# Second feed-forward stage as seven block products

## The reference

```
def swiglu(u, w13, w2):
    a, b = jnp.split(u @ w13, 2, axis=-1)
    return (jax.nn.silu(a) * b) @ w2

def half_ffn(h, shift, scale, gate, g_pre, g_post, w13, w2):
    u = modulate(rmsnorm(h, g_pre), shift, scale)
    return h + 0.5 * gate * rmsnorm(swiglu(u, w13, w2), g_post)
```

## Time and profile before

| | |
|---|---|
| median of three runs | 2694.71 us |
| the profiled execution | 2693.38 us, span 2691.5 us |
| TensorE busy | 2550.4 us, 95% |
| VectorE busy | 1322.4 us, 49% |
| GpSimd busy | 1311.0 us, 49% |
| ScalarE busy | 850.0 us, 32% |
| mean granted TensorE clock | 0.975 |

### The profile page before, as it was taken

The page is one execution under the profiler, slowest core; times in us unless marked ns, Lnnn a source line. Parts: engine busy times, 40 slices in busy tenths (PEclk is TensorE's granted clock), DMA queues, the critical chain, the costliest instruction groups (busy, mean ns, idle before and its releaser), DMA issues. The chain is left out here.

```text
span 2691.5 us, 36342 instructions
## 1 busy us (share of the span) xinstructions
PE 2550.4 (95%) x14266; PEld 2208.8 (82%) x14266; DVE 1322.4 (49%) x1908; ACT 850.0 (32%) x1373; POOL 1311.0 (49%) x499
## 2 busy tenths in 40 slices
PE   7999999998998999998999998989989999979997
PEld 5899998887898888786888877879878898867775
DVE  6445663468664652035111225364445144359997
ACT  5333331234212422024100114334422011128774
POOL 1444544542642067774778775655537776620000
PEclk8999999999999999998999998999999999989998
DMA  7664423314211022231222224110012322539994
GB/s 281 231 245 153 154 98 127 123 66 167 76 66 35 20 94 94 94 129 63 100 84 106 95 93 178 67 62 1 1 66 106 127 88 85 200 141 401 372 374 167
DMA packets 59197, 352.10 MB, mean 131 GB/s; under 512 B 7236, under 2 KB 8388, under 8 KB 26352
## 3 DMA queue, kind: packets, MB, share of 16 engines
q1 hardware_dynamic: 57472, 344.39, 34.2%
q0 software_dynamic: 1584, 5.78, 0.5%
HBM read 323.13 MB, written 30.72 MB: 131 GB/s over the span
## 5 line engine op out<-in xcount | busy, mean ns | idle before, releaser
L186 POOL TENSOR_TENSOR whi<-raw,one_col 128x2048 fp32r<-128x2048 f32 (+2 forms) x135 | 445.3, 3298 | 666.3 <-PE bank L206 559.6
L189 POOL TENSOR_TENSOR wlo<-raw,whi 128x2048 fp32r<-128x2048 f32 (+2 forms) x135 | 578.3, 4284 | 10.6
L4443 DVE TENSOR_TENSOR moe_wl<-moe_raw,moe_wh 128x2048 fp32r<-128x2048 f32 x84 | 189.6, 2284 | 3.4 <-ACT moe_wh L4377 3.0
L4377 ACT ACTIVATE moe_wh<-moe_raw 128x2048 fp32r<-128x2048 f32 x84 | 160.0, 1913 | 36.8 <-PE bank L4355 19.3
L204 PE MATMUL bank<-uh_b,whi 128*128 128x512 f32 x352 | 139.1, 395 | 7.8 <-DVE ul_b L1063 6.8
L205 PE MATMUL bank<-ul_b,whi 128*128 128x512 f32 x352 | 138.3, 393 | 0.0
L206 PE MATMUL bank<-uh_b,wlo 128*128 128x512 f32 x352 | 138.1, 392 | 0.0
L4292 POOL DMA_INDIRECT out_dram<-moe_y,moe_rows x7 | 6.7, 950 | 258.5 <-DVE moe_y L4507 258.5
L204 PE MATMUL bank<-fa_hh,whi 128*128 128x512 f32 (+1 forms) x352 | 119.5, 340 | 3.3 <-DVE fa_hl L1761 3.3
L205 PE MATMUL bank<-fa_hl,whi 128*128 128x512 f32 (+1 forms) x352 | 119.4, 339 | 0.0
L206 PE MATMUL bank<-fa_hh,wlo 128*128 128x512 f32 (+1 forms) x352 | 119.0, 338 | 0.0
(11 more groups left out here) (701 smaller groups left out, 7364.4 us busy)
## 6 DMA issues: line engine op xcount, KB each, us to landing
moe_raw<-moe_w_dram SPq DMA_DIRECT2D x84, 1024.0 KB, 7.3
cond_ring<-w_ada_dram SPq DMA_DIRECT2D x27, 1024.0 KB, 8.9
raw<-gu_a_dram SPq DMA_DIRECT2D x22, 1024.0 KB, 5.0
raw<-gu_b_dram SPq DMA_DIRECT2D x22, 1024.0 KB, 4.8
raw<-wqkv_dram SPq DMA_DIRECT2D x12, 1024.0 KB, 4.8
raw<-dn_a_dram SPq DMA_DIRECT2D x16, 704.0 KB, 4.0
raw<-dn_b_dram SPq DMA_DIRECT2D x16, 704.0 KB, 4.0
n_ada<-w_ada_dram SPq DMA_DIRECT2D x9, 1024.0 KB, 21.6
```

The source lines that it names most:

```text
L186: e.nc.gpsimd.tensor_tensor(e.whi[p][:, 0:f], e.raw[p][:, 0:f], e.one_col[:, 0:1].to_broadcast([P, f]), ALU.mult).then_inc(e.w_hi, 1)
L189: e.nc.gpsimd.tensor_tensor(e.wlo[p][:, 0:f], e.raw[p][:, 0:f], e.whi[p][:, 0:f].bitcast(F32), ALU.subtract).then_inc(e.w_split, 1)
L4377: nc.scalar.activation(wh[s % RING_W][:, :], raw[s % RING_RAW][:, :], ACT.Copy).then_inc(hi_done, 1)
L4443: nc.vector.tensor_tensor(wl[s % RING_W][:, :], raw[s % RING_RAW][:, :], wh[s % RING_W][:, :].bitcast(F32), ALU.subtract).then_inc(lo_done, 1)
```

## The change

The second stage is written as a new function, `ffn_seven_b`, with its own object of class `Seven`:

- The stream order is gu_b0, gu_b1, dn_b0, dn_b1. Slots 0 to 2 stay as they are, the other 19 are seven block products of 256 columns.
- Three weight sums are left on GpSimd (`pool_sums` is 3); the fourth is on VectorE (`dve_sum`). All seven low parts are on VectorE (`pool_lo` is empty).
- The norm writes its tiles over the residual XR (`over_x`), so that the token blocks are whole and can be summed in place.
- The first 11 gated tiles stay in SBUF (`fb_kept`, where `fb_hl` comes to lie), the other 11 go to `hid_b` in memory by way of two buffers, and come back tile by tile while the last down slot of the first half frees `fb_hl`.
- The kept tiles are split when the last gate-and-up slot is in work; the first down slot's weights are split by ScalarE and VectorE.

```diff
-          ("gu_b0", HTILES, 16), ("dn_b0", 8, HTILES), ("gu_b1", HTILES, 16), ("dn_b1", 8, HTILES),
+          ("gu_b0", HTILES, 16), ("gu_b1", HTILES, 16), ("dn_b0", 8, HTILES), ("dn_b1", 8, HTILES),
...
+        if over_x:
+            self.u = [self.x[:, k, 0:w] for k in range(KT)]
+        self.nu = len(self.u)
...
+            if self.pool_lo:
+                dve.wait_ge(self.lo_pool, 2 * i + 2)
...
+    def last_sum(self, eng, i):
+        return eng.tensor_tensor(self.block(i, 0), self.block(i, 1), self.s[1][:, :], ALU.subtract)
+    def dve_sum(self, dve, i):
+        dve.wait_ge(self.s_ready, self.pool_sums * i + 3)
+        dve.wait_ge(self.lo_part, self.lo_count(i, 0))
+        self.last_sum(self.e.nc.vector, i).then_inc(self.s_last, 1)
     def pool_slot(self, pool, i):
-        e, G, g, s = self.e, self.e.nc.gpsimd, self.first + i, self.s
+        e, G, g, s, n = self.e, self.e.nc.gpsimd, self.first + i, self.s, self.pool_sums
         a11, a12, a21, a22 = (self.block(i, n) for n in range(4))
         pool.wait_ge(e.w_landed[g % 2], 16 * (g // 2) + 16)
         if i:
-            pool.wait_ge(self.lo_part, 4 * (i - 1) + 4)
+            pool.wait_ge(self.lo_part, self.lo_count(i - 1, 3))
+            if n < 4:
+                pool.wait_ge(self.s_last, i)
         G.tensor_tensor(s[0][:, :], a21, a22, ALU.add).then_inc(self.s_ready, 1)
-        pool.wait_ge(self.s_ready, 4 * i + 1)
+        pool.wait_ge(self.s_ready, n * i + 1)
         G.tensor_tensor(s[1][:, :], s[0][:, :], a11, ALU.subtract).then_inc(self.s_ready, 1)
         G.tensor_tensor(a21, a11, a21, ALU.subtract).then_inc(self.s_ready, 1)
-        pool.wait_ge(self.s_ready, 4 * i + 3)
-        pool.wait_ge(self.lo_part, 4 * i + 1)
-        G.tensor_tensor(a11, a12, s[1][:, :], ALU.subtract).then_inc(self.s_ready, 1)
-        self.pool_unit(pool, i, 4)
-        self.pool_unit(pool, i, 5)
+        if n == 4:
+            pool.wait_ge(self.s_ready, n * i + 3)
+            pool.wait_ge(self.lo_part, self.lo_count(i, 0))
+            self.last_sum(G, i).then_inc(self.s_ready, 1)
+        for j in self.pool_lo:
+            self.pool_unit(pool, i, j)
...
+def ffn_seven_b(e, name, uh, ul, y, hid_at, v_at, front, sums, seven):
...
+        def _(sp):
+            front.sp(sp)
+            fed = sp_span[0]
+            for k in range(HTILES):
+                g = u0 + HTILES + k
+                feed_sp(e, sp, (fed, g + 3))
+                fed = g + 3
+                sp.wait_ge(e.acc_free, g + 1)
+                sp.dma_start(hid[k], tile(g)).then_inc(stored[k % 2], 16)
+            feed_sp(e, sp, (fed, d0_end + 2))
+            for r in range(2):
+                sp.wait_ge(stored[r], 16 * ((HTILES + 1 - r) // 2))
+            for k in range(HTILES):
+                sp.wait_ge(*((k_freed, k + 1) if k < HTILES - 1 else (e.slot_done, d0_end)))
+                sp.dma_start(kept[:, k, :], hid[k]).then_inc(tile_in[k], 16)
+            feed_sp(e, sp, (d0_end + 2, sp_span[1]))
+        @block.gpsimd
+        def _(pool):
+            pool.wait_ge(e.w_split, u0 + 2)
+            feed_pool(e, pool, (u0 + 2, s0))
+            for i in range(seven.n):
+                seven.pool_slot(pool, i)
+            pool.wait_ge(e.w_split, d0 + 1)
+            feed_pool(e, pool, (d0 + 1, pool_span[1]))
...
+            for g in range(u0, s0):
+                pe_slot_begin(e, pe, g)
+                ready = (lambda k: pe.wait_ge(front.lo_ready, k + 1)) if g == u0 else None
+                pe_feature_major(e, g % 2, KT, 2, uh, ul, False, ready=ready).then_inc(e.slot_done, 1)
+            for i in range(seven.n):
+                seven.pe_slot(pe, i)
...
+            slots(pe, d0, d0 + 1, lambda *s: down_slot(*s, half=0))
+            slots(pe, d0 + 1, d0_end - 1, down_slot)
+            slots(pe, d0_end - 1, d0_end, lambda *s: down_slot(*s, freed=True))
+            slots(pe, d1, d1 + 1, lambda *s: down_slot(*s, half=1))
+            slots(pe, d1 + 1, d1_end, down_slot)
...
+            for m in (3, 2, 4):
+                seven.act_token(act, m)
+            silu_slot(u0)
+            seven.act_token(act, 1)
+            silu_slot(u0 + 1)
+            for j in range(4):
+                seven.act_unit(act, 0, j)
+            silu_slot(u0 + 2)
+            for j in range(4, 7):
+                seven.act_unit(act, 0, j)
+            for i in range(seven.n):
+                g = s0 + i
+                more = i < end
+                if more:
+                    seven.act_unit(act, i + 1, 0)
+                free_tile(act, g)
+                seven.act_copy(act, i, tile(g))
+                if more:
+                    for j in range(1, 4):
+                        seven.act_unit(act, i + 1, j)
+                    seven.act_silu(act, i, 0)
+                    for j in range(4, 7):
+                        seven.act_unit(act, i + 1, j)
+                    seven.act_silu(act, i, 1)
+            high_tiles(0, 0, 3)
+            act.wait_ge(e.w_landed[d0 % 2], 16 * (d0 // 2) + 16)
+            act.wait_ge(seven.multiplied, 6 * end + 4)
+            nc.scalar.activation(e.whi[d0 % 2][:, 0:f], e.raw[d0 % 2][:, 0:f], ACT.Copy).then_inc(e.w_hi, 1)
+            seven.act_silu(act, end, 0)
+            high_tiles(0, 3, 6)
+            seven.act_silu(act, end, 1)
+            high_tiles(0, 6, HTILES)
+            high_tiles(1, 0, HTILES)
...
+            seven.dve_tokens(dve)
+            for n, m in enumerate((3, 2, 4)):
+                seven.dve_token(dve, m, n + 1)
+            mul_slot(u0)
+            seven.dve_token(dve, 1, 4)
+            mul_slot(u0 + 1)
+            for j in range(4):
+                seven.dve_unit(dve, 0, j)
+            seven.dve_sum(dve, 0)
+            mul_slot(u0 + 2)
+            for j in range(4, 7):
+                seven.dve_unit(dve, 0, j)
+            for i in range(seven.n - 1):
+                t = tile(s0 + i)
+                for n in range(3):
+                    seven.dve_unit(dve, i + 1, n)
+                    seven.dve_mix(dve, i, n, t)
+                seven.dve_unit(dve, i + 1, 3)
+                seven.dve_sum(dve, i + 1)
+                for j in (4, 5):
+                    seven.dve_unit(dve, i + 1, j)
+                seven.dve_mix(dve, i, 3, t)
+                seven.dve_gate(dve, i, 0, t)
+                seven.dve_unit(dve, i + 1, 6)
+                seven.dve_mix(dve, i, 4, t)
+                seven.dve_gate(dve, i, 1, t)
+            t = tile(u_end - 1)
+            for n in range(3):
+                seven.dve_mix(dve, end, n, t)
+            low_tiles(0, 0, 2)
+            dve.wait_ge(e.w_hi, d0 + 1)
+            dve.wait_ge(e.w_split, d0)
+            nc.vector.tensor_tensor(e.wlo[d0 % 2][:, 0:f], e.raw[d0 % 2][:, 0:f], e.whi[d0 % 2][:, 0:f].bitcast(F32),
+                                    ALU.subtract).then_inc(e.w_split, 1)
+            low_tiles(0, 2, 3)
+            seven.dve_mix(dve, end, 3, t)
+            seven.dve_gate(dve, end, 0, t)
+            low_tiles(0, 3, 4)
+            seven.dve_mix(dve, end, 4, t)
+            seven.dve_gate(dve, end, 1, t)
+            low_tiles(0, 4, HTILES)
...
+            low_tiles(1, 0, HTILES)
+            slots(dve, d0_end - 1, d0_end, out_slot(0))
+            slots(dve, d1, d1_end, out_slot(1), straight=True)
...
-                    (e.bank[2 * (START["gu_b0"][0] % 2) + 1],), joint=False)
+                    (e.bank[2 * (START["gu_b0"][0] % 2) + 1],), joint=False, over_x=True)
+    seven = Seven(e, "sw", T, n3, XR, MAIN + 107520, uh, ul, (MAIN + 77824, MAIN + 123904, MAIN + 132096),
+                  (MAIN + 86016, MAIN + 88064), TMP + 14336, START["gu_b0"][0] + 3, START["gu_b1"][1], (0, 1, 4, 5, 2, 3),
+                  (), 3)
     Y2 = at("Y2", [P, KT, T], 107520)
     with one_block(e):
         post_sum = SquareSum(e, "s4", Y2, 6, sums.pick)
-        ffn(e, "fb", "gu_b", "dn_b", T, HTILES, uh, ul, Y2, MAIN + 32768, front=n3, sums=post_sum)
+        ffn_seven_b(e, "fb", uh, ul, Y2, MAIN + 32768, TMP, n3, post_sum, seven)
```

More of the change, by code:

```diff
@@ L926, with __init__ @@
 class JoinedNorm:
-    def __init__(self, e, name, sums, uh, ul, pre, g, ring_at, r1, r2, store=None, joint=True, third=None):
+    def __init__(self, e, name, sums, uh, ul, pre, g, ring_at, r1, r2, store=None, joint=True, third=None, over_x=False):
         self.e, self.st, self.sums, self.w, self.y, self.x = e, Stage(e, name), sums, sums.w, sums.y, sums.x
@@ L1425, in banks @@
     def banks(self, i):
-        return [self.e.bank[self.RING[(4 * i + n) % 6]][:, 0:HW] for n in range(4)]
+        return [self.e.bank[self.ring[(4 * i + n) % 6]][:, 0:self.hw] for n in range(4)]
     def dve_tokens(self, dve):
```

143 lines of the change are left out of this document (114 added, 29 removed).

## The result

The changed kernel takes 2701.45 us (median of nine runs, 2700.88 to 2707.38) against 2694.61 for the kernel before (nine runs, 2691.99 to 2699.07) on the same chip: 1.0032 times as long, 95% interval 1.0024 to 1.0041. It is slower by 0.3%; 2701.4 was forecast. The ratio is not that of the two medians: it stands for 8.6 us, where the medians lie 6.8 us apart. A second series of runs of the same two kernels (e0) gave 1.0036, 1.0022 to 1.0049.

What follows compares the result with a forecast made beforehand. The stage was taken to be bound by TensorE's matmuls. Terms -16.6 + 7.5 + 4.3 + 4.5 + 5.1 + 1.9 = +6.7 us on the median of 2694.71 gave 2701.4 us, range 2684 to 2715.

Steps and rivals of the forecast that it cites:

- 19 slots of seven products: Gate-and-up slots: 84 matmuls of 256 columns replace 48 of 512, 10.06 us a slot for 10.88, 15.6 us saved.
- wait for wlo: TensorE's one 1.0 us wait for a low part from GpSimd, after down slots, goes: 1.0 us saved.
- start, stall: Start of the second stage: GpSimd holds VectorE's token sums and low parts; TensorE waits 7.5 us for the first slot's product.
- turns, stall: Turns to the down slots, both halves: GpSimd's splits hold VectorE's low parts of gated tiles; TensorE stands 4.3 and 4.5 us.
- clock, three times: Behind the start's and both turns' stalls TensorE's granted clock drops, 1.7 us lost each, 5.1 us in all.
- semaphores: Block's end: 27 more semaphore clears on GpSimd, 0.072 us each, delay its first split by 1.9 us; a clock drop possible.
- TensorE-bound loop: The 19 slots: VectorE needs 9.5 to 9.9 us with waits, under TensorE's 10.06, so it costs 0.
- rival 3: Steady loop: VectorE, waiting behind GpSimd's sums, needs up to 10.9 us a slot; nothing saved, 2717 us; chance 0.2.
- Rival 1: Start and turns: GpSimd and VectorE are not in each other's way, no stalls, 2680 us; chance 0.13.
- rival 2: Turns cost what they do in the first stage, 2.1 us or less each, clock falls once: 2693 us; chance 0.15.

Runs made afterwards that it cites:

- e0: The changed kernel once more, unaltered, for a second profile: 2704.99 us, 1.0036 to before.
- e5: The changed kernel with the last weight sum and low parts 4 and 5 of every seven-product slot on GpSimd, not VectorE: 2727.43 us, 1.0125 to before.
- e4: The changed kernel with high and low parts of the first six gated tiles made one in each of six earlier slots: 2705.13 us, 1.0045 to before.
- e1: The changed kernel with the first ordinary slot's SiLU and product put ahead of the third token sum and the token parts: 2698.47 us, 1.0010 to before.
- e6: The changed kernel with the eleven gated tiles read back early from memory into space of their own: 2704.05 us, 1.0044 to before.
- e8: The kernel of e6 with the high parts of both splits at turn 2 on ScalarE, not GpSimd: 2702.46 us, 1.0031 to before.
- e3: The changed kernel with the high parts of two weight blocks (turn 1, ahead of turn 2) on ScalarE, not GpSimd: 2701.97 us, 1.0020 to before.
- e7: The changed kernel with four edits together: e1, the turn 1 part of e3, e4 and e6: 2690.52 us, 0.9989 to before.
- e9: The kernel of e7 plus e8's high parts, two low parts ahead of turn 1's last gate, one semaphore for eleven tiles: 2683.97 us, 0.9971 to before.
- e2: The kernel before with 27 more semaphores, used by nothing, so only their clears are added: 2697.81 us, 1.0012 to before.
- e10: The changed kernel with GpSimd's splits of three weight blocks at the turns made in four pieces per high and low part: 2700.76 us, 1.0032 to before.

## Why the prediction was right

The time was within its range and its sign right, but the sum was luck in part: by the marks of the two profiles, the stretch from the start of the stage to the last split (2353.35 before) is 10.5 us longer in e0 and 13.7 in the first profile, where 6.7 were forecast; the ratio with its interval says 6.5 to 11. That the forecast of 2701.4 is the measured median to 0.1 us is chance. Step by step, stalls from start to start:

| step | forecast | measured |
|---|---|---|
| 19 slots of seven products | -15.6 | -14.8 |
| wait for wlo | -1.0 | -1.3 |
| start, stall | +7.5 | +7.3 |
| turns, stall | +4.3, +4.5 | +4.1, +4.1 |
| clock, three times | +5.1 | 2.4 + 1.9 + 1.8 = +6.1 |
| semaphores | +1.9 | +2.1, and +1.4 of clock |
| not foreseen | | +1.0 in the norm behind the stage |

The first five rows make +5.5 us, as much as the stage is longer (354.96 against 349.44).

- *TensorE-bound loop* (rival 3 was the doubt): right. No gap in 192 us, with VectorE at 90%. e5 comes to the rival's price (10.99 us a slot) in another way, with more work on GpSimd; how near the changed kernel is to it isn't measured, but e4 put another 0.6 us on VectorE in six slots without loss.
- *Start*: the laid-out queue was right to 0.4 us (product at 1275.88, forecast 1276.2), and e1 took the stall away by order alone.
- *Turns*: the stall was right to 0.4 us. The two waits of the forecast (1.25 and 3.05) are there at each turn, 1.3 and 2.8. For turn 2 I named the trip through memory as what leaves only two or three tiles ready; e6 shows that taking it out alone gains nothing, and with two of GpSimd's instructions gone as well (e8) the whole turn goes.
- *Clock*: 1.0 us too small in sum. The 1.7 us for each stall, carried over from the first stage, was close at the turns (1.9 and 1.8, of which 0.2 to 0.5 are the first intervals behind the stalls) and too low at the start (2.4). A fixed price for a stall doesn't hold either: with the same two stalls slot d0 takes 13.46 us in the changed kernel, 14.70 in e1 and 14.45 in e5. Turn 2 takes 14.3 to 14.8 us in e3, e4 and e6. It is not simply that what is won at one place is lost at the next: in e1, e3 and e4 something had been won ahead of the dearer turn, in e5 and e6 nothing, and in e7 the start and turn 1 were shortened and turn 2 lost no more to the clock. What decides it stays open. With no stall left (e9) the clock is 1.00 in all four windows shown.
- *Semaphores*: the clears as forecast; the drop of the clock behind them, which the text left as a possibility, happens in the changed kernel and in e2.
- *Not foreseen*: 1.0 us more between the stage's last split and the next weights (1613.82 to 1636.8 against 1608.05 to 1630.03), at a lower clock (0.55 against 0.61) with the same work. It is there in four of the profiles (the changed kernel's, e0's, e1's and e5's), and in no other; what decides it stays open. So does the spread of a single kernel's runs over 6 us or more, of which the two profiles of the changed kernel show the parts at 505 to 519 and at 1658 to 1680 us, away from the stage.

Rival 1 (no mutual hold) is refuted by the start above (4.50 and 5.51 us for token sums that take 1.22 alone) and by e10, rival 2 (turns as cheap as in the first stage) by the 4.1 us of stall in each.
